# Dilated attention groups in the order 16, 4, 1, the last group's records kept in SBUF, and row maxima negated as they are reduced

## What is computed

```python
DIL_PATTERNS = ((128, 1), (512, 4), (2048, 16))      # (window, dilation), 4 heads of 64 each

def dilated_prompt_group(q, k, v, window, dilation):   # for each group g
    ...                                    # tokens t, t+dilation, ... form sub-sequences, blocks of 128
    kk = with_prev(to_sub(k))              # a block of queries sees its own and the previous block of keys
    sc = einsum(qb, kk) * (e ** -0.5)
    m = max(sc);  ex = exp(sc - m);  den = sum(ex)
    o = einsum(ex, vv) / den;  lse = m + log(den)

def combine_groups(outs, lses):            # per token and head slot, over the three groups
    w = softmax(stack(lses)); return sum(w * outs)

h = h + w_out(sigmoid(gA) * (A @ w_o_mla) + sigmoid(gB) * (B @ w_o_dil))
```

## Time and profile before

| | |
|---|---|
| median of 3 runs | 2558.02 us (2555.55 to 2566.73) |
| the profiled execution, its own time | 2559.34 us |
| its span | 2557.2 us |
| PE busy | 2470.5 us |
| DVE busy | 1106.0 us |
| ACT busy | 580.7 us |
| POOL busy | 844.2 us |
| mean granted TensorE clock | 0.986 of 2.4 GHz |

### The profile page before, as it was taken

How to read it: one execution, slowest core, us unless ns; L and a number is a source line. 1 busy time by engine, 2 the same in 40 slices (tenths; PEclk the granted TensorE clock), 3 DMA queues, 4 the chain that set the end, 5 groups by cost and what they waited for, 6 DMA issues and landing times. The chain is left out here.

```text
span 2557.2 us, 40664 instructions
## 1 busy us (share of the span) xinstructions
PE 2470.5 (97%) x16119; PEld 2356.0 (92%) x16119; DVE 1106.0 (43%) x1944; ACT 580.7 (23%) x1332; POOL 844.2 (33%) x435
## 2 busy tenths in 40 slices
PE   7999999999999999999999889899999999999996
PEld 7999999999999998999766667899999999999996
DVE  7522232332346764311566455755732323222226
ACT  6200000000013441211556344113400000000002
POOL 1233344433345541433000121443044433344433
PEclk9999999999999999999999899999999999999998
DMA  4212222122223432421211355552112211111111
GB/s 167 83 65 94 73 89 79 65 87 73 96 73 123 145 114 102 143 94 73 73 46 45 97 215 177 168 166 80 61 69 78 85 43 48 50 50 50 42 42 66
DMA packets 85311, 229.45 MB, mean 90 GB/s; under 512 B 8889, under 2 KB 47330, under 8 KB 84034
## 3 DMA queue, kind: packets, MB, share of 16 engines
q1 hardware_dynamic: 79066, 207.90, 24.0%
q10 hardware_dynamic: 6088, 19.23, 1.9%
HBM read 196.69 MB, written 74.39 MB: 106 GB/s over the span
## 5 line engine op out<-in xcount | busy, mean ns | idle before, releaser
L805 PE MATMUL ps<-u_hi,w_hi 128*128 128x352 f32 (+1 forms) x2880 | 928.9, 323 | 23.6 <-DVE w_lo L1898 12.8
L806 PE MATMUL ps<-u_lo,w_hi 128*128 128x352 f32 (+1 forms) x2880 | 922.5, 320 | 0.0
L807 PE MATMUL ps<-u_hi,w_lo 128*128 128x352 f32 (+1 forms) x2880 | 920.5, 320 | 0.0
L708 POOL TENSOR_TENSOR w_hi<-raw,zero 128x1024 fp32r<-128x1024 f32 x170 | 323.1, 1900 | 1312.7 <-PE ps L805 1136.4
L805 PEld LDWEIGHTS ps<-u_hi,w_hi 128*128 128x128 f32 x2880 | 543.2, 189 | 28.7 <-DVE w_lo L1898 13.1
L806 PEld LDWEIGHTS ps<-u_lo,w_hi 128*128 128x128 f32 x2880 | 543.9, 189 | 0.9
L807 PEld LDWEIGHTS ps<-u_hi,w_lo 128*128 128x128 f32 x2880 | 543.3, 189 | 0.0
L711 POOL TENSOR_TENSOR w_lo<-raw,w_hi 128x1024 fp32r<-128x1024 f32 x170 | 416.7, 2451 | 13.4
L2041 DVE TENSOR_TENSOR h<-ps,silu 128x352 f32<-128x352 f32 (+1 forms) x120 | 61.9, 516 | 679.6 <-PE ps L807 679.6
L2048 DVE SCALAR_TENSOR_TENSOR x<-ps,x 128x352 f32<-128x352 f32 (+1 forms) x528 | 267.9, 513 | 185.9 <-PE ps L807 184.4
L805 PE MATMUL ps<-h_hi,w_hi 128*128 128x352 f32 (+1 forms) x1056 | 338.6, 321 | 1.8 <-DVE x L2048 1.7
(11 more groups left out here) (289 smaller groups left out, 2660.6 us busy)
## 6 DMA issues: line engine op xcount, KB each, us to landing
raw<-in_wstream SPq DMA_DIRECT2D x186, 512.0 KB, 3.3
out_win_out<-in_cache_win SPq DMA_DIRECT2D x23, 1424.0 KB
latn<-in_cache_mla SPq DMA_DIRECT2D x128, 80.0 KB, 1.9
scratch_gates<-stage ACTq DMA_DIRECT2D x16, 516.0 KB, 2.6
out_win_out<-in_cache_win SPq DMA_DIRECT2D x7, 1168.0 KB
kv_d<-in_cache_win SPq DMA_DIRECT2D x24, 256.0 KB, 7.6
sgt<-scratch_gates SPq DMA_DIRECT2D x16, 352.0 KB, 3.8
scratch_x_mid<-x SPq DMA_DIRECT2D x1, 4128.0 KB, 22.2
```

Of the source, the lines that this page charges most:

```text
L708: nc.gpsimd.tensor_tensor(hi, raw[:, s % RAW], zero[:].to_broadcast([P, UW]), ALU.add).then_inc(w_hi_done, 1)
L805: a = mm(out, wh, xh, start=start, stop=False)
L806: mm(out, wh, xl, start=False, stop=False)
L807: return a, mm(out, wl, xh, start=False, stop=stop)
```

## The change

1. The groups run in the order 2, 1, 0, so dilation 16 first and dilation 1 last. Steps 0 to 7 are now all single; 16 is single and 17 to 23 are double. Slots of q, k, v follow the order (`group_slot`).
2. Group 0's records are neither stored nor loaded: with dilation 1 they are already in token order, in the 8 slots of `rec`. SP stores 16 records in place of 24 and loads 2 x 1056 KB in place of 3.
3. SP's order: weights and records are loaded after the 16 stores, not within the steps; the first two gate tiles (`sgt`) are loaded before the last two weight units; `gate_a` has other addresses for this.
4. PE: 6 `early` tiles, half 0 of the combination, 2 `early` tiles, half 1, 1 `early` tile. DVE: weights of the combination first, then the products, each followed by an `early`.
5. `row_max`, `gmax`: the reduction negates (`negate=True`) and the instruction behind it is gone (64 + 24). The scale is put into q beforehand: in MLA by the root's `scale` and `eps_q`, in the dilated branch by the scale of the copy L1632 and by SCALAR_TENSOR_TENSOR in place of TENSOR_TENSOR at L2122 (18 of 36).

```diff
-        GSTEPS = [(g, n) for g in range(NG) for n in range(8)]
+        GORDER = (2, 1, 0)
+        GSTEPS = [(g, n) for g in GORDER for n in range(8)]
+        N_REC = 8 * (NG - 1)
+        records = [recs[:, GORDER.index(g)] if g > 0 else rec[:] for g in range(NG)]
+        CB_ORDER = ((2, 1, 0), (0, 2, 1))
...
-            for s, (g, n) in enumerate(GSTEPS):
+            for s, (g, n) in enumerate(GSTEPS[:N_REC]):
                 sp.wait_ge(go_kept, s + 1)
                 if s == 8:
-                    load_group(2)
-                if s == DD_OWN + 1:
-
-                    sp.wait_ge(dd_v, N_DDV)
-                    for unit in (U_MIX, U_MIX + 1):
-                        load_unit(unit, unit % RAW)
+                    load_group(GORDER[2])
                 sp.dma_start(io["rec"][g][group_tile(g, n)], rec[:, s % NREC]).then_inc(rec_stored[s % NREC], 16)
-                if s == DD_OWN + 2:
-                    load_records(0)
-                    load_records(1)
-                if s == DD_OWN + 3:
-                    for m in range(EARLY):
-                        sp.dma_start(gate_a[m][:], io["gates"][m]).then_inc(ga_landed, 16)
+            sp.wait_ge(dd_v, N_DDV)
+            for unit in (U_MIX, U_MIX + 1):
+                load_unit(unit, unit % RAW)
+            load_records(2)
+            load_records(1)
+            for m in range(EARLY):
+                sp.dma_start(gate_a[m][:], io["gates"][m]).then_inc(ga_landed, 16)
...
-                V.tensor_reduce(st_max[:, 4 * (s % 2):4 * (s % 2) + 4],
+                V.tensor_reduce(rec[:, s % NREC, 256:260],
                                 ps[:, 2 * (s % 2):2 * (s % 2) + 2, :].rearrange("p a (j c) -> p (a j) c", j=2)[:, :, 0:w],
-                                axis=AX, op=ALU.max).then_inc(gmax_done, 1)
-                dve.wait_ge(gmax_done, s + 1)
-                V.tensor_scalar(rec[:, s % NREC, 256:260], st_max[:, 4 * (s % 2):4 * (s % 2) + 4], -DSCALE, None, ALU.mult
-                                ).then_inc(gneg_done, 1)
+                                axis=AX, op=ALU.max, negate=True).then_inc(gneg_done, 1)
...
-            for j in range(NT * EARLY):
+            def early(j):
...
+            for j in range(6):
+                early(j)
             for half in range(2):
-                for g in range(NG):
-                    pe.wait_ge(cb_v, N_CBW + NG * half + g + 1)
+                for i, g in enumerate(CB_ORDER[half]):
+                    pe.wait_ge(cb_v, N_CBW + NG * half + i + 1)
...
+                for j in ((6, 7), (8,))[half]:
+                    early(j)
...
-            for j in range(4):
-                early(j)
-
             c = Tally(cb_v)
-            dve.wait_ge(recs_landed, 48)
-            nm = [recs[:, g, :, 256:260] for g in range(NG)]
+            dve.wait_ge(recs_landed, 32)
+            dve.wait_ge(gp_done, 24)
+            nm = [records[g][:, :, 256:260] for g in range(NG)]
```

More of the change, by code:

```diff
@@ L662, in _ @@
                         sp.wait_ge(g_mulB, j - 1)
-                    sp.dma_start(sgt[:, j % 2, :, 0:TILES[t][1]],
-                                 io["gates"].rearrange("(a m) p t -> m p a t", a=2)[m][:, :, tile(t)]
-                                 ).then_inc(sg_landed[j % 2], 16)
+                        load_gates(j)
                 if 2 <= m < KD - 2:
@@ L1365, in gvalues @@
                                   gprobsT[:, s % 2, 256 * j + k * P:256 * j + k * P + P],
-                                  v_g[g % 2][:, kt, h * HD:(h + 1) * HD], start=k == 0, stop=k == (1 if two else 0))
+                                  v_g[group_slot(g)][:, kt, h * HD:(h + 1) * HD], start=k == 0, stop=k == (1 if two else 0))
                 last.then_inc(go_ready, 1)
@@ L1631, in _ @@
                         a, b = 32 * q, 32 * (q ^ 1)
-                        last = A(swapped[a:a + 32, e % 2, 0:w], ps[b:b + 32, bank, 0:w], ACT.Copy)
+                        last = A(swapped[a:a + 32, e % 2, 0:w], ps[b:b + 32, bank, 0:w], ACT.Copy,
+                                 scale=DSCALE if (c - 4) % 4 < 2 else 1.0)
                     last.then_inc(act_read, 1)
@@ L1666, in _ @@
                     bank = t if k == 0 else (3, 0, 1)[t]
-                    A(dst, ps[:, bank, 0:TILES[t][1]], ACT.Sqrt, bias=eps[:], scale=1.0 / (256 if k == 0 else P)
+                    A(dst, ps[:, bank, 0:TILES[t][1]], ACT.Sqrt, bias=(eps_q if k == 0 else eps)[:],
+                      scale=1.0 / (256 * MSCALE ** 2 if k == 0 else P)
                       ).then_inc(small_std, 1)
@@ L1740, in exponential @@
                 A(probs[S % 2][:, 0:w], ps[:, 2 * (S % 2):2 * (S % 2) + 2, :].rearrange("p a c -> p (a c)")[:, 0:w],
-                  ACT.Exp, bias=st_negm[:, S % 8:S % 8 + 1], scale=MSCALE,
+                  ACT.Exp, bias=st_negm[:, S % 8:S % 8 + 1],
                   accum_out=st_den[:, S % 8:S % 8 + 1]).then_inc(probs_done, 1)
@@ L1810, in decode_exp @@
                 da.by(A(dprobs[:, r], ps[:, 0:4, :].rearrange("p a c -> p (a c)"), ACT.Exp,
-                        bias=s_stat[:, r, 3:4], scale=MSCALE, accum_out=s_stat[:, r, 4:5]))
-                n = da.by(A(s_stat[:, r, 5:6], s_stat[:, r, 0:1], ACT.Exp, bias=s_stat[:, r, 3:4], scale=MSCALE))
+                        bias=s_stat[:, r, 3:4], accum_out=s_stat[:, r, 4:5]))
+                n = da.by(A(s_stat[:, r, 5:6], s_stat[:, r, 0:1], ACT.Exp, bias=s_stat[:, r, 3:4]))
                 assert n == DMA_EXP[r]
@@ L1841, in dsampled @@
                     pd = p_d[:].rearrange("p g c -> p (g c)")
-                    dda.by(A(pd, pd, ACT.Exp, bias=n_d[:, 5:6], scale=DSCALE, accum_out=n_d[:, 8:9]))
-                    dda.by(A(n_d[:, 10:13], n_d[:, 0:3], ACT.Exp, bias=n_d[:, 5:6], scale=DSCALE,
-                             accum_out=n_d[:, 9:10]))
+                    dda.by(A(pd, pd, ACT.Exp, bias=n_d[:, 5:6], accum_out=n_d[:, 8:9]))
+                    dda.by(A(n_d[:, 10:13], n_d[:, 0:3], ACT.Exp, bias=n_d[:, 5:6], accum_out=n_d[:, 9:10]))
             def gcopy_odd(s):
@@ L2121, in _ @@
                         V.tensor_copy(r_col[:], ps[:, 7, 0:9]).then_inc(r_col_kept, 1)
-                    V.tensor_tensor(rot[:, e % 2, 0:w], ps[:, bank, 0:w], rope_c[:, tile(t)], ALU.mult
-                                    ).then_inc(dve_read, 1)
+                    if (c - 4) % 4 < 2:
+                        V.scalar_tensor_tensor(rot[:, e % 2, 0:w], ps[:, bank, 0:w], DSCALE, rope_c[:, tile(t)],
+                                               ALU.mult, ALU.mult).then_inc(dve_read, 1)
+                    else:
+                        V.tensor_tensor(rot[:, e % 2, 0:w], ps[:, bank, 0:w], rope_c[:, tile(t)], ALU.mult
+                                        ).then_inc(dve_read, 1)
                     V.tensor_tensor(swapped[:, e % 2, 0:w], swapped[:, e % 2, 0:w], rope_s[:, tile(t)], ALU.mult
@@ L2377, in dsampled @@
                     dve.wait_ge(dd_v, n)
-                    n = d.by(V.tensor_scalar(n_d[:, 5:6], n_d[:, 13:14], -DSCALE, None, ALU.mult))
+                    n = d.by(V.tensor_scalar(n_d[:, 5:6], n_d[:, 13:14], -1.0, None, ALU.mult))
                     assert n == N_DDX, n
@@ L2481, in _ @@
             assert n == N_CBW, n
-            j = 4
+            j = 0
             for half in range(2):
                 part = slice(4 * half, 4 * half + 4)
-                for g in range(NG):
+                for g in CB_ORDER[half]:
                     n = c.by(V.tensor_tensor(comb[:, half, g].rearrange("p n (j e) -> p n j e", j=GH),
-                                             recs[:, g, part, 0:256].rearrange("p n (j e) -> p n j e", j=GH),
+                                             records[g][:, part, 0:256].rearrange("p n (j e) -> p n j e", j=GH),
                                              wgt[:, g, part].unsqueeze(3).to_broadcast([P, 4, GH, HD]), ALU.mult))
-                    if j < NT * EARLY:
-                        early(j)
-                        j += 1
+                    early(j)
+                    j += 1
             for k in range(4):
@@ L2497, in _ @@
                                 ).then_inc(od_done, 1)
+                if k == 1:
+                    early(6)
+                    early(7)
             dve.wait_ge(od_hi_done, 5)
@@ L2500, in _ @@
                             ).then_inc(od_done, 1)
+            early(8)
             def mlower(j):
```

81 lines of the change are left out of this document (46 added, 35 removed).

## The result

| kernel | median us | runs | ratio to before, 95% interval | span of the profiled execution |
|---|---|---|---|---|
| before | 2557.82 | 18 | | 2557.2 |
| changed | 2567.89 (2563.13 to 2570.15) | 18 | 1.0040 (1.0033 to 1.0047) | 2565.6 |

The change costs 10 us: inside the forecast's range of 2551 to 2571 and within 0.5% of before, but three times the sum of +3.2, and at the value that rival C gave (2566 to 2571).

The account below looks back on a forecast made before the run. It took PE to bound MLA and dilated steps 8 to 23, transfers steps 0 to 8. Terms -1.0 + 0 - 1.8 + 8.9 - 2.9 = +3.2 us on 2559.34 gave 2562.5, a median of about 2561, range 2551 to 2571.

Parts of the forecast that it names:

- rival C: Dilated steps: PE's pause costs more than its length, matmuls go on at 1.2 GHz, tail stays bad; 2566 to 2571, chance 0.18.
- What bounds each stage: PE bounds MLA, transfers hold dilated steps 0 to 8, PE paces steps 8 to 23, DVE the main loop's start.
- Steps 8 to 15: Dilated steps after the pause: 1 us from less work to make up, 0.8 from the missing negation; -1.8 us.
- Steps 16 to 23: Last dilated steps: seven single steps become double, +14.0 us, the bad end goes, 5.1 less; +8.9 us.
- End of the steps to the main loop: Merge, last copy to first gated product: PE works without a wait, 29.4 us in place of 32.3; -2.9 us.
- A: The forecast: seven double steps paid outside the transfers' shadow, the merge gives a part back; 2561 us, chance 0.50.
- Loads in another order: SP's weights, records and gates after the 16 stores come in time, main loop's loads as before; 0, bounds 2 either way.
- Negation: In MLA, removing DVE's negating instructions gains 1 us for the short steps at the start; -1 us, bounds 0 and 3.
- B: Faster: the first store lands earlier, so the ninth dilated step's maximum starts earlier; 2554 to 2547 us, chance 0.27.
- D: Negation carries further in MLA: the chain over DVE sets its pace, giving 8 us; 2553 us, chance 0.05.

Follow-up runs that it names:

- e4: The changed kernel with the first eight records stored from ACT's queue rather than SP's: 2562.03 us, ratio 1.0010 to the kernel before.
- e6: The changed kernel with 78 matmuls that nobody reads added in PE's gaps: 2562.95 us, ratio 1.0025 to the kernel before.
- e2: The kernel before with the order of the groups alone changed (16, 4, 1), all 24 records still through memory: 2566.88 us, ratio 1.0025.
- e3: The changed kernel with the groups in the order 4, 16, 1: 2566.11 us, ratio 1.0023 to the kernel before.
- e7: The changed kernel with the first eight records stored from ACT's queue and unread matmuls added in PE's remaining gaps: 2560.76 us, ratio 1.0011 to before.
- e1: The kernel before with the negation alone (row maxima negated by the reduction, scales folded in beforehand): 2559.25 us, ratio 0.9998.

## Why the prediction was right in range and wrong in size

*What bounds each stage* was read rightly. The loads begin 1.0 us sooner, the first store is issued 0.9 us sooner and `gmax(8)` waits for it, 7.3 us, where I said over 10. The eight single steps ahead of it took 25.7 us (33.0 less the wait) where I had 18: PE's clock was 0.71 over that stretch. This cost nothing, as it lay in the shadow. e4 shows the cause of the wait by taking it away.

*Steps 8 to 15, the term "-1.8 us", is the step that failed.* I put "net of matmuls at the lower clock after the pause" at a gain. It measured +1.6, 3.4 off. With the clock kept (e6) the stretch is 27.8, a shift of -2.2. So the work was counted rightly and the clock was mis-sized: 3.8 us for this pause in this execution, and at most 1.7 in e2's (29.5 against 27.8).

*Steps 16 to 23, the term "+8.9 us"*, measured +11.1; with the clock kept +9.4. The forecast took the bad end away altogether. POOL's stretched instruction is gone, as expected, but the last sixteen value matmuls and some transposes ahead of them still fell to 1.2 GHz: 1.8 us. In e3 and e4 they didn't, so this part can come or stay away with the same code there.

*End of the steps to the main loop, the term "-2.9 us"*, measured -1.3; with the clock kept 29.4 against 32.3, just -2.9. Two instructions of the weights, 1.77 us at 1605.75 and 2.27 at 1607.75, ran beside POOL, long as feared, and were covered. POOL's two, and PE's combination, which follows six early tiles without a gap:
```profile
1605.57 1.89 POOL L722 TENSOR_TENSOR w_hi<-raw,zero 128x1024 fp32r<-128x1024 f32 x1 [3.55 <-PE ps L820]
1607.54 2.42 POOL L725 TENSOR_TENSOR w_lo<-raw,w_hi 128x1024 fp32r<-128x1024 f32 x1
```
```profile
1618.09 5.52 PE L1425 MATMUL ps<-ident,comb 128*128 128x128 f32 x48
```
By the Trainium skill (SBUF — State Buffer, "Who interferes with whom") a `tensor_tensor` with both inputs in SBUF contends with a GpSimd instruction that reads SBUF. This case agrees: the two DVE instructions end within 0.1 us of POOL's, against 0.18 to 0.19 us for the same shape where POOL is quiet. (In the earlier trace rows the 2.48 us are three instructions, of which one took 2.27; the forecast's sum doesn't change by it.)

*Taken together*: at the first gated product the forecast was +3.2, the changed kernel has +10.5, and the changed kernel with its clock kept has 1628.4 - 1625.1 = +3.3. The sum of A was that of a kernel at full clock. That it comes within 0.1 us is luck: both are single executions, and before's lies 1.5 us above its median. Rival C, with chance 0.18, named the mechanism and the place, and its 2566 to 2571 holds the median; its sizes, 5 us behind the pause and 5 in the tail, were too large against 3.8 and 1.8, with 1.6 in the merge that it didn't have. I should have priced the low clock behind the pause into A: the changed kernel, e2, e3 and e4 all show it behind their gaps. Only its length varies.

*Loads in another order, 0*: the main loop is 2.2 us shorter, a gain that the forecast hadn't. It is why the span grows by 8.4 and not 10.5. Its cause stays open. e2, whose loads are the old ones, has 64.9 and so most of the gain; e3 and e7, which have the new loads, have 65.9 and 64.0. Starting later isn't the cause either, since e3 starts last and e7 first of these.

*Negation, -1*: the loads begin 1.0 us sooner in the changed kernel and 1.4 in e1, but also 1.5 sooner in e2, which has no negation. So the -1.0 that was measured isn't shown to be the negation's. From the first to the last row maximum MLA takes 169.3 us in before, 168.0 in e2, and 167.4 to 167.6 in all ten kernels that negate. e1 shows no change of the total by it. *B and D* didn't occur.

*What stays open*: e6's median is 5.5 us above before's though its profiled execution is only 2.0 above. About 1.9 of the difference is that before's profiled execution lies above the median of e6's session, 1.6 that e6's lies below its own. The stretches are therefore known to 1 or 2 us only. Nor is the part of the change beyond the order told apart from nothing.

By the Trainium skill (TensorE: Matmul & The Clock Gate, "Why this matters for your kernels") gaps between matmuls cost throughput after them, since the array returns to its lower clock. This case agrees: 3.8 us after a pause of 7 us in the changed kernel, at most 1.7 in e2.

## What to carry to other kernels

Price a pause of TensorE at its length plus the slow matmuls behind it: here 3.8 us behind 7 us in one execution, at most 1.7 behind 6.9 in another. A stretch that waits for transfers hides work for nothing, so put the longest steps into it, and ask what stands in the queue ahead of the store that frees the first buffer. And before moving work out of a slow end, look whether something else arrives at that end anyway: in the old order 5.7 us of steps were slack, in the new one PE is busy for 30.8 of the 30.9 us of the merge, and what the steps lose comes through to its end.

## What the hardware did that I had not expected

The clock falls without any long pause. In e4 the first value matmuls of the single steps, at 1498.7, take 1.72 us for eight, in place of 1.08, and from 1490 to there PE has no gap above 1.41 us. The maxima of steps 3 to 6 then come 4.15 us apart, almost without a gap of PE:
```profile
1494.60:1515.00 20.40, 18.85 (x112) 15.44 (x113) 10.60 (x18) 10.74 (x53) 7.50 (x5) 0.61 1.03 388
```
PE is busy 18.85 of 20.4 us, at clock 0.61. At 1.2 GHz its work fills the step; back at 2.4 GHz the next two maxima come 2.7 and 3.0 us apart. Single steps and double steps can so take the same time, and a step's duration read at one clock can't be carried to a place where the clock is another.

It also falls with no gap at all. In e3 PE is busy for 18.60 of the 18.60 us from 1561.4 to 1580, and still:
```profile
1572.33 1.04 PE L1358 MATMUL ps<-ident,gprobs 128*128 128x128 f32 x8
...
1577.14 3.26 PE L1379 MATMUL ps<-v_g,gprobsT 128*128 128x64 f32 x16
```
Sixteen such value matmuls take 1.89 us at the high clock, and the eight transposes behind them take 1.91 in place of the 1.04 shown. Ahead of the slow ones stand 32 small matmuls of the sampled queries, of 32 columns each. The changed kernel has the same ones and keeps 1.00 from 1559.8 to 1595.3. So the place of a low clock can differ from run to run, and the granted clock has to be read beside every stretch that is compared.
